# Thirteen DRAM transfers moved forward on GpSimd's queue, products that start on rounded weights, and four reordered places at the start and the end of a transformer kernel

## What is computed

```
def swiglu(h, w_gate, w_up, w_down):
    return (jax.nn.silu(h @ w_gate) * (h @ w_up)) @ w_down

def first_block(x, ...):
    h = rms_norm(x, g_pre_mix)
    x = x + rms_norm(chunk_relpos_attention(h, w_qkv, w_o, rel_bias), g_post_mix)
    h = rms_norm(x, g_pre_ffn)
    return x + rms_norm(swiglu(h, w_gate, w_up, w_down), g_post_ffn)

def hybrid_layer(x, ...):
    proj = rms_norm_2(x, norm_g) @ w_in
    ...                                     # y_a, y_b, y_c, y_d from slices of proj
    branch_d = jnp.einsum('nbsw,nwd->bsnd', ys, w_branch)
    g = jax.nn.sigmoid(gates.reshape(bsz, s, N_BRANCH, d))
    merged = jnp.sum(g * branch_d, axis=2)
    return x + merged @ w_out

reference = rms_norm_2(hybrid_layer(first_block(x)), final_g)
```

## Time and profile before

| | us |
|---|---|
| median of three runs | 1248.23 |
| the profiled execution | 1246.92 |
| its span, first to last instruction | 1245.0 |
| TensorE matmuls busy | 1234.0 (99%) |
| VectorE busy | 874.7 (70%) |
| ScalarE busy | 657.7 (53%) |
| GpSimd busy | 87.6 (7%) |

### The profile page before, as it was taken

How to read it: one execution, slowest core, us unless ns; L and a number is a source line. 1 busy time by engine, 2 the same in 40 slices (tenths; PEclk the granted TensorE clock), 3 DMA queues, 4 the chain that set the end, 5 groups by cost and what they waited for, 6 DMA issues and landing times.

```text
span 1245.0 us, 19430 instructions
## 1 busy us (share of the span) xinstructions
PE 1234.0 (99%) x7425; PEld 1084.9 (87%) x7425; DVE 874.7 (70%) x1557; ACT 657.7 (53%) x1230; POOL 87.6 (7%) x137
## 2 busy tenths in 40 slices
PE   9999999999999999999999999999999999999997
PEld 7887777899999998888888888788899999998986
DVE  5377776697766688888574788674786775656687
ACT  5366676455445455666553333563366765353644
POOL 1000000010010100001100000010000000000001
PEclk9999999999999999999999999999999999999999
DMA  7259888167668755654625887777988887555541
GB/s 254 103 170 252 219 233 237 66 237 222 152 207 233 213 162 171 222 213 172 201 68 173 230 258 228 205 208 205 312 265 260 250 257 248 216 174 198 214 159 68
DMA packets 41852, 253.26 MB, mean 203 GB/s; under 512 B 5272, under 2 KB 6428, under 8 KB 13856
## 3 DMA queue, kind: packets, MB, share of 16 engines
q1 hardware_dynamic: 26952, 161.05, 35.7%
q0 software_dynamic: 11808, 85.99, 28.6%
q10 hardware_dynamic: 3000, 4.99, 1.3%
HBM read 241.51 MB, written 81.80 MB: 260 GB/s over the span
## 4 chain that ended last, share of the span: by engine, by line
PE 96%; DVE 2%; issue 1%; ACT 1%; POOL 0%; POOLq 0%; DVEq 0%; ACTq 0%
PE bank L2422 23%; PE bank L2424 23%; PE bank L2423 23%; PE sc L2422 4%; PE sc L2424 4%; PE sc L2423 4%; PE sc L2598 3%; PE tp L2607 2%; PE ob L2664 1%; PE ob L2622 1%; PE bank L2539 1%; PE bank L2548 1%; PE bank L2529 1%; PE ob L2422 1%; PE tp L2422 1%
## 5 line engine op out<-in xcount | busy, mean ns | idle before, releaser
L1536 DVE TENSOR_TENSOR w_lo<-w_raw,w_hi 128x512 fp32r<-128x512 f32 (+1 forms) x417 | 300.8, 768 | 131.0 <-ACT w_hi L925 130.1
L925 ACT ACTIVATE w_hi<-w_raw 128x512 fp32r<-128x512 f32 (+1 forms) x417 | 262.9, 688 | 139.9 <-PE bank L2424 92.2
L2422 PE MATMUL bank<-xT_hi,w_hi 128*128 128x256 f32 (+1 forms) x928 | 319.7, 344 | 0.3
L2424 PE MATMUL bank<-xT_hi,w_lo 128*128 128x256 f32 (+1 forms) x928 | 309.3, 333 | 0.0
L2423 PE MATMUL bank<-xT_lo,w_hi 128*128 128x256 f32 (+1 forms) x928 | 308.9, 333 | 0.0
L2422 PEld LDWEIGHTS bank<-xT_hi,w_hi 128*128 128x128 f32 x928 | 176.3, 190 | 20.3 <-issue 4.6
L2424 PEld LDWEIGHTS bank<-xT_hi,w_lo 128*128 128x128 f32 x928 | 176.1, 190 | 17.7
L2423 PEld LDWEIGHTS bank<-xT_lo,w_hi 128*128 128x128 f32 x928 | 176.5, 190 | 15.4 <-issue 1.0
L2422 PE MATMUL bank<-act_hi,w_hi 128*128 128x256 f32 (+1 forms) x400 | 124.5, 311 | 0.0
L2423 PE MATMUL bank<-act_lo,w_hi 128*128 128x256 f32 (+1 forms) x400 | 123.4, 308 | 0.0
L2424 PE MATMUL bank<-act_hi,w_lo 128*128 128x256 f32 (+1 forms) x400 | 123.3, 308 | 0.0
(11 more groups left out here) (368 smaller groups left out, 2363.1 us busy)
## 6 DMA issues: line engine op xcount, KB each, us to landing
w_raw<-in_weights SPq DMA_DIRECT2D x84, 1024.0 KB, 5.0
sum_dram<-in_weights POOLq DMA_DIRECT2D x54, 1024.0 KB, 8.8
w_raw<-sum_dram SPq DMA_DIRECT2D x34, 1024.0 KB, 4.8
sum_dram<-sum_dram POOLq DMA_DIRECT2D x18, 1024.0 KB, 7.2
arena<-in_weights SPq DMA_DIRECT2D x8, 1024.0 KB, 9.4
act_f<-in_weights POOLq DMA_DIRECT2D x6, 1024.0 KB, 10.5
arena<-in_weights POOLq DMA_DIRECT2D x4, 1024.0 KB, 11.5
act_lo<-act_lo SPq DMA_DIRECT2D x24, 128.0 KB, 5.7
```

What stands on the lines that cost most here:

```text
L925: nc.scalar.activation(w_hi[SPLIT_AT[b]][:, cols], w_raw[SLOT[b]][:, cols], ACT.Copy)\
L1536: nc.vector.tensor_tensor(w_lo[SPLIT_AT[b]][:, cols], w_raw[SLOT[b]][:, cols], w_hi[SPLIT_AT[b]][:, cols].bitcast(F32), ALU.subtract).then ...
L2422: nc.tensor.matmul(ps, hi_l, hi_r, start=first, stop=False, skip_group_check=onto)
L2424: return nc.tensor.matmul(ps, lo_l, hi_r, start=False, stop=last, skip_group_check=onto)
```

## The change

On **GpSimd**: six transfers of the sums are issued behind the last up quad, ahead of the roots of the second pair of norms; one behind the triangle mask; four behind the mask of the mixing weights; one each behind the first and second score mask. 33 stay at the end. On **TensorE**: in `feature_chunk`, the down products and, in `up_quad` and `gate_quad`, the first half h = 0, a matmul that needs only `w_hi` waits for `w_rounded`, and only the third waits for `w_split`; for h = 0 all matmuls with `w_hi` come first. One number of `SMALL_AT` changes from 5 to 6. At the **start** VectorE scales the second tile ahead of rounding the first. At the **end** the right half of tile 3 goes from VectorE's `norm_out` to GpSimd's `gain_out` and ScalarE's `scale_out`, tile 3 is stored whole by SP, and the root of tile 2 stands between GpSimd's gains.

```
-OUT_POOL_GAINS = [(0, 0), (1, 0)]
+OUT_POOL_GAINS = [(0, 0), (1, 0), (3, 1)]
-SMALL_AT = (((1, 3, 4, 6, 7), (1, 3, 5, 7)), ((0, 3, 6), (0, 4)), ((0, 4), (0, 4)), ((), ()))
+SMALL_AT = (((1, 3, 4, 6, 7), (1, 3, 6, 7)), ((0, 3, 6), (0, 4)), ((0, 4), (0, 4)), ((), ()))
...
+            step(weight_sums, 6)
             reciprocal_roots("post2", "pre2")
             pool.wait_ge(x_updated, 2 * TT)
             nc.gpsimd.memset(tri, 1.0).then_inc(tri_made, 1)
...
+            step(weight_sums, 1)
             reciprocal_roots("ln")
             reciprocal_roots("c")
...
+            step(weight_sums, 4)
             for t in range(1, TT):
                 pool.wait_ge(score_added, IDX_H * t)
...
+                if t < TT - 1:
+                    step(weight_sums, 1)
             step(weight_sums, 8 * len(GROUPS))
...
+            pool.wait_ge(merged_split, left_count("s3", 1))
+            gain_out(0, 0)
+            pool.wait_ge(out_gained, OUT_GAINS.index((2, 1)) + 1)
+            gain_out(1, 0)
+            root("final", 2)
+            gain_out(3, 1)
+            for t in OUT_TILES[1:]:
                 root("final", t)
...
-            scale_out(0, 2)
+            scale_out(0, 2, slice(0, D))
             squares_out("finalb", 0, last_add(0, 1), right)
             squares_out("finalb", 1, last_add(1, 1) - 1, slice(W, W + W // 2))
+            scale_out(1, 3, right)
             squares_out("finalc", 1, last_add(1, 1), slice(W + W // 2, D))
-            scale_out(1, 0)
-            scale_out(2, 1)
+            scale_out(2, 0)
+            scale_out(3, 1)
...
             variance("pre0", 1, D)
+            scale_first(1, 0)
             dve.wait_ge(cols_made, 1)
             round_first(0)
-            scale_first(1, 0)
...
             variance_last("finalb", var_begun)
-            norm_out(3, 1)
+            norm_out(0, 1)
             variance_last("finalc", var_done)
-            norm_out(0, 1)
             norm_out(1, 1)
...
+            def product_high(ps, hi_w, hi_x, lo_x, first):
+
+                nc.tensor.matmul(ps, hi_w, hi_x, start=first, stop=False, skip_group_check=True)
+                nc.tensor.matmul(ps, hi_w, lo_x, start=False, stop=False, skip_group_check=True)
+
+            def product_rest(ps, lo_w, hi_x, last):
+
+                return nc.tensor.matmul(ps, lo_w, hi_x, start=False, stop=last, skip_group_check=True)
...
                     if arriving and k * PARTS % kc < PARTS:
+                        pe.wait_ge(w_rounded, PARTS * b + k * PARTS // kc + 1)
+                    w = slice(BLK // kc * k + P * c, BLK // kc * k + P * c + P)
+                    product_high(bank[e % 4][:, tok], w_hi[SPLIT_AT[b]][:, w], rhs_hi[:, k, tok], rhs_lo[:, k, tok], k == 0)
+                    if arriving and k * PARTS % kc < PARTS:
                         pe.wait_ge(w_split, PARTS * b + k * PARTS // kc + 1)
...
                         if r == 0:
+                            pe.wait_ge(w_rounded, PARTS * o + k - lo + 1)
```

More of the change, by code:

```diff
@@ L1031, in round_first @@
                 act.wait_ge(cols_made, 1)
+                act.wait_ge(xT_rounded, half_at("pre0", t, 0))
                 act.wait_ge(xpose_done, half_at("pre0", t, 0) + 1)
@@ L2928, in gate_quad @@
                         place = gate_bank[f][GATE_BANK[i]][h]
+                        if h == 0:
+                            for m in range(2):
+                                for k in range(KW):
+                                    if m == 0:
+                                        pe.wait_ge(w_rounded, PARTS * o + k + 1)
+                                    at = W * k + P * m
+                                    product_high(place[:, ST * m:ST * m + ST], w_hi[SPLIT_AT[o]][:, at:at + P], x_hi[name][:, k, :], x_lo[name][:, k, :],
+                                                 i in GATE_OPENS and m == 0 and k == 0)
+                                    if m == 0 and k == 0 and f in (1, 2):
+                                        step(dsa, 1)
+                                    if f == 0 and i == G_22 and (h, m, k) in QLAT_AT:
+                                        step(small, 1)
+                            for m in range(2):
+                                for k in range(KW):
+                                    if m == 0:
+                                        pe.wait_ge(w_split, PARTS * o + k + 1)
+                                    at = W * k + P * m
+                                    last = product_rest(place[:, ST * m:ST * m + ST], w_lo[SPLIT_AT[o]][:, at:at + P], x_hi[name][:, k, :], k == KW - 1)
+                            last.then_inc(quad_full, 1)
+                            continue
                         for m in range(2):
                             for k in range(KW):
-                                if h == 0 and m == 0:
-                                    pe.wait_ge(w_split, PARTS * o + k + 1)
                                 at = W * k + P * (2 * h + m)
```

72 lines of the change are left out of this document (43 added, 29 removed).

## The result

| | us |
|---|---|
| before, median of 10 runs | 1246.99 (1246.34 to 1250.9) |
| changed, median of 10 runs | 1252.41 (1250.46 to 1254.98) |
| ratio, 95% interval | 1.0039, 1.0031 to 1.0048 |
| profiled execution of the changed kernel, its span | 1252.11, 1250.4 |

The forecast was 1246.6, with a range of 1243.5 to 1251. The changed kernel is above the range. Its runs also scatter over 4.5 us, those of the kernel before mostly over 2.

A forecast was written before the change was run, and what follows sets the result against it. TensorE was taken as the bound, its matmuls busy 1234.0 of 1245.0 us. Gains 0.4 + 0.81 + 0.54 + 0.4 = 2.15, less 0.5 lost, gave 1.65: 1248.23 - 1.65 = 1246.6 us, range 1243.5 to 1251.

The forecast's parts named there:

- The moved transfers: Six transfers beside the second FFN matrix's weight loads: a loss of 0.5 us, bounds 0 and 5.7.
- the cycle: One raw weight buffer's rounding, split and next load, second FFN matrix: 8.3 us, against 10.0 for TensorE's two blocks.
- the second reserve: Second FFN matrix: a rest's first half is ready 1.7 to 3.1 us before TensorE needs it, plus 0.45.
- loads come late: Rival, second FFN matrix: loads take 8.2 us, TensorE loses 5.7, total 1251.8; chance 0.15.
- two reserves: Second FFN matrix: 1.7 us in hand in the buffer's cycle, and TensorE's further slack; counted against late loads.
- Queue of GpSimd: Second FFN matrix: the sixth transfer issued at about 506 to 529, roots 34 us in hand; no loss.
- late roots: Rival, second FFN matrix: transfers over 17.9 us delay GpSimd's first root; at 19, 5.6 us lost, about 1251.7; chance 0.03.
- Products that start on rounded weights: Three waits, at 255.50, 491.47 and 532.60, removed: 0.81 us gained, 0.57 of it in the second FFN matrix.
- The start: Second tile's transposes lose their wait for VectorE's scaling: 0.4 us gained, bounds 1.0 and a loss of 0.3.
- The small product: Index score's first matmul at 642.99: three more matmuls ahead of it remove its holdup; 0.54 us gained.
- The end: Last root takes 0.55 instead of 0.99 us: 0.4 gained, bounds 0.8 and a loss of 0.3.
- the lock: Shared SBUF port: two-input VectorE and SBUF-reading GpSimd instructions exclude each other; frees last root (0.4), start only 0.1 to 0.3.

The follow-up runs named there:

- e13: Changed kernel with each of the three additions among the six transfers cut by columns into four parts of 256 KB, issued one after another; 1262.27 us.
- e1: Changed kernel without the six transfers beside the second FFN matrix, all else kept; 1244.87 us.
- e4: Kernel before with only the split waits, the new end and both the first and second index scores three matmuls later; 1245.54 us.
- e5: Changed kernel with three of the six transfers beside the second FFN matrix, the other three after its roots; 1246.01 us.
- e2: Kernel before with nothing but the six transfers put ahead of the second norm's roots; 1255.34 us.
- e8: Kernel before with five further 128x512 copies on ScalarE ahead of its copy of the third product's bank, no transfer moved; 1252.69 us.
- e9: Kernel before with nine further copies on ScalarE ahead of its copy of the third product's bank, no transfer moved; 1256.20 us.
- e12: Changed kernel, the same program, timed and profiled a second time; 1253.69 us.
- e14: Changed kernel with each of the three additions among the six transfers cut by columns into halves of 512 KB; 1252.09 us.
- e10: Changed kernel without the six transfers and with the first index score also three matmuls later; 1244.28 us.
- e3: Changed kernel with ScalarE's first copy of the third product's bank put ahead of its rounding of the ninth weight block; 1252.15 us.
- e15: Changed kernel with each of the three additions among the six transfers cut by rows into quarters of 32 rows; 1250.73 us.
- e7: Changed kernel with the three additions among the six transfers made plain copies of the same size; 1247.30 us.
- e16: Changed kernel with each of the three additions among the six transfers cut by rows into halves of 64 rows; 1248.56 us.

## Why the prediction was wrong, by its own steps

- **The moved transfers: wrong, the whole error.** Forecast 0.5 lost, measured 7.5. The failed step is "Beside sums, loads take 6.9 ... At 6.9 the cycle is 10.4 ... which the second reserve holds: no loss". By the medians the load time was near (7.2 and 7.5), but the ten loads from 475.62 to 526.43 took 6.7 to 10.8, 7.7 on average. With 7.4 the same sum gives a cycle of 10.9, 0.9 too long over 5.1 cycles, less 2.5 of reserve: 2.1 lost. With 7.7 it gives 11.2, 1.2 too long over 5 cycles, less 2.5: 3.5 lost. The waits measured in the profile come to 4.55 and the clock to 1.7. So the load was sized too small by a median from another stretch, a cycle that a late load made 12.4 long (503.45 to 515.81) could not be made up, and the clock was left out; about 1 us of the waits stays open, and whether the reserve of 2.5 was the wrong part of it is not shown. Nearer rows stood in the trace of before: three loads issued 0.5, 1.0 and 1.4 behind an addition (at 935.66, 1003.06 and 801.34) took 12.3, 9.7 and 9.1, about as long as the addition. The earlier trace rows give an addition 8.5 at the median and 11.0 once.
- **No term had the clock.** Behind 526.15 it cost 1.7 of the 6.0; no row shown ahead of the prediction had a clock that fell.
- **Rival "loads come late": it is what happened**, in the place and with the sign given to it, and its time, 1251.8, is within 0.6 of the median. That closeness is partly luck: it took loads of 8.2 where they took 7.7, had no clock, and took off 0.54 for the score, which did not come. Its chance of 0.15 was too small: the "two reserves" counted against it did not last beyond about 500 us.
- **Queue of GpSimd: right.** Six transfers by about 530, the roots not late; the price of late roots was seen in e13 alone. The seven other moved transfers cost nothing that the profiles show: from the last product of the second matrix to the last matmul it is 670.00 in e1 and 670.33 before.
- **Products that start on rounded weights: right, a little small.** In the second matrix 102.52 went to 101.75 (e1, e4, e5), 0.77 for 0.57 forecast; at 255.50 the wait is gone, 0.2 for 0.24.
- **The start: right.** A matmul that starts at 227.78 in the profile before starts at 227.87 to 228.37 in the four other profiles with the old start. With the new one it starts at 227.18 to 227.64 in twelve profiles and at 228.02 in that of the changed kernel: by the medians 0.5 earlier, for 0.4 forecast. The changed kernel's profile is the odd one, 0.24 later than the one before, since its first weights landed late: ScalarE's first rounding began at 8.70 there, 7.65 before, and the first product waited for it.

```profile
7.75 0.49 DVE L1584 TENSOR_SCALAR arena<-x_sb,rstd 128x512 f32<-128x512 f32 x1 [0.67 <-POOL rstd L788]
...
8.70 0.63 ACT L934 ACTIVATE w_hi<-w_raw 128x512 fp32r<-128x512 f32 x1 [1.84 <-DMA w_raw<-in_weights]
```

- **The small product: wrong place.** Forecast 0.54, measured nothing. The step at the first score is 0.77 in the profile before and 0.62 in that of the changed kernel, but it is 0.62 or 0.63 in e2, e8 and e9 too, which have the old number, and 0.77 in e12 and e14, which have the new one. The change moves the second score's product; the first, whose holdup is in the earlier trace rows, stands behind the same six matmuls as before. "Three matmuls more ahead of it" misread the table. With the first one moved too, the whole holdup went (e4), and the median fell by another 0.6 (e10 against e1; 0.4 if each is set against the kernel before beside it).

```profile
648.21 0.40 PE L2443 MATMUL bank<-xT_hi,w_lo 128*128 128x512 f32 x1
648.83 0.36 PE L2857 MATMUL sc<-act_hi 128*128 128x256 f32 x1 [0.22 <-DVE act_lo L2083]
```

- **The end: right.** The last root is 0.55 long for 0.99, and from the last matmul to the end of the span it is 7.25 for 7.60: 0.35 of the 0.4. The root with no two-input norm beside it is as short as the lock that the prediction cited from the Trainium skill (page "SBUF — State Buffer", section "Who interferes with whom") would have it. No run took only that norm away, but the profiles bear the lock out further than the prediction read them. In the four with the old end (before, e2, e8, e9) the last root ends 0.40 to 0.42 behind the end of that norm. And VectorE's scaling of the second tile, where it began beside a GpSimd instruction, ends 0.28 or 0.29 behind that one's end: beside the subtraction before (9.95 and 9.67), in e2, e4 and e9, and beside the cast in e3 and e5, where it took 0.81 for 0.49 (in e8 only 0.14 us of the two overlapped, and nothing was lost):

```profile
7.67 0.61 POOL L792 CAST w_hi<-w_raw 128x512 fp32r<-128x512 f32 x1
7.75 0.81 DVE L1586 TENSOR_SCALAR arena<-x_sb,rstd 128x512 f32<-128x512 f32 x1 [0.67 <-POOL rstd L788]
```

So the row at 9.04 fits a wait for GpSimd's end in whole, not "in part only", though the scaling has one tensor input and the prediction worded the rule for two. The start gained 0.4 in e3 and e5 even so. The changed kernel's last root:

```profile
1244.96 0.55 POOL L784 TENSOR_TENSOR rstd<-var,minus_half 128x1 f32<-128x1 f32 x1 [1.04 <-DVE var L2415]
```

The gains without the transfers were forecast at 2.15; e1 has 2.9 by the medians and 2.0 between the profiled spans, without the 0.54 of the score.

## What to carry to other kernels

Before a transfer is put beside a stream of loads, look at each load's own slack (from landing to first use) and at the longest load that the transfer can make, not at mean busy shares or a median: here a load issued just behind a long transfer mostly landed with it, the delay was handed on to the next load of the same buffer, and TensorE paid for some waits twice, in the wait and in the clock. Start such work where the ring of buffers is full and stop where its reserve ends: here three transfers cost 1.1 and six 7.5. Test the parts of a bundle one by one, since gains of 2.9 were hidden here under one loss.

## What the runs showed of the hardware

- An addition into DRAM by DMA, 1 MB, took 8.6 to 12.5 us from issue to landing beside the loads of the second FFN matrix, where a plain copy mostly took 5 to 8 (9.9 in e15, 9.7 in e14); a quarter of it takes 8.2 cut by columns (all 128 rows) and 4.9 cut by rows.
- Loads of half the columns took 3.7 alone, whole ones 4.8, and both 9 to 11 just behind an addition (8.8 and 6.0 in two cases of e3).
- The clock fell behind waits of TensorE of 2.1, 2.5 and all from 2.9 to 5.1 us, and behind 1.9 with 0.5 soon after; it did not behind others of 1.9, 2.0 and 2.5.
- Where a VectorE and a GpSimd instruction met, the one that began second ended a fixed time behind the end of the first: VectorE's scaling 0.28 to 0.29 (six profiles), GpSimd's last root 0.40 to 0.42 (four profiles), GpSimd's first cast 0.46 to 0.47 (e1, e7, e10, e12, e13, e16).
- Stretches with late loads come with a scattering time: 1249.6 to 1257.3 in e12_changed_again, 1244.0 to 1245.4 in e10_best, which has none.
